# High parts of the first twelve weight blocks: from GpSimd to ScalarE, in a two-layer decoder trunk

## The reference

```python
hn = rms_norm(h, mix_norm[0])
proj = hn @ w_in                      # 1024 x 3584: x, y, q, k, v side by side
x_br, y_br, q, k, v = split(proj)
xc = causal_depthwise_conv(x_br, conv_w, conv_b)      # width 4, per channel
r = sigmoid(block_diag_linear(xc, wa, ba))            # the gates: 4 blocks of 256 x 256
i = sigmoid(block_diag_linear(xc, wx, bx))
```

## Time and profile before

| | us |
|---|---|
| median of 3 runs | 1297.19 (1297.11 to 1297.23) |
| the profiled execution | 1297.3 |
| its span in the trace | 1295.5 |
| TensorE busy | 1286.3 |
| VectorE busy | 921.9 |
| ScalarE busy | 532.5 |
| GpSimd busy | 258.7 |

### The profile page before, as it was taken

How to read it: one execution, slowest core, us unless ns; L and a number is a source line. 1 busy time by engine, 2 the same in 40 slices (tenths; PEclk the granted TensorE clock), 3 DMA queues, 4 the chain that set the end, 5 groups by cost and what they waited for, 6 DMA issues and landing times.

```text
span 1295.5 us, 19991 instructions
## 1 busy us (share of the span) xinstructions
PE 1286.3 (99%) x7554; PEld 1115.4 (86%) x7554; DVE 921.9 (71%) x1458; ACT 532.5 (41%) x1124; POOL 258.7 (20%) x295
## 2 busy tenths in 40 slices
PE   9999999999999999999999999999999999999998
PEld 7778778888888998899988878888888998899986
DVE  8997857446689984388955778557789983489842
ACT  5247356113533560056622347425433550166512
POOL 3111253311422002100021126413321002000010
PEclk9999999999999999999999999999999999999999
DMA  6333323233333333333233332132333323333232
GB/s 236 102 106 113 91 66 98 66 98 98 114 98 98 114 98 98 98 115 98 87 110 114 106 106 69 50 98 88 108 98 98 114 91 94 99 126 98 82 98 98
DMA packets 96701, 130.73 MB, mean 101 GB/s; under 512 B 5312, under 2 KB 61888, under 8 KB 96608
## 3 DMA queue, kind: packets, MB, share of 16 engines
q1 hardware_dynamic: 94976, 127.42, 32.0%
q10 hardware_dynamic: 1632, 2.05, 0.6%
HBM read 124.67 MB, written 2.10 MB: 98 GB/s over the span
## 4 chain that ended last, share of the span: by engine, by line
PE 91%; DVE 5%; issue 2%; DMA 1%; ACT 0%; POOL 0%; SPq 0%; DVEq 0%; POOLq 0%; ACTq 0%
PE ps L784 17%; PE ps L788 16%; PE ps L787 16%; PE ps L942 8%; PE ps L941 8%; PE ps L940 8%; DVE xc L1689 1%; PE ps L1426 1%; PE ps L1427 1%; PE ps L1423 1%; PE ps L1256 1%; PE ps L1272 1%; PE ps L1285 1%; DVE w_lo L1455 1%; PE ps L1145 1%
## 5 line engine op out<-in xcount | busy, mean ns | idle before, releaser
L706 POOL TENSOR_SCALAR w_hi<-raw 128x1024 fp32r<-128x1024 f32 x161 | 184.6, 1147 | 933.9 <-PE ps L942 367.3
L1455 DVE TENSOR_TENSOR w_lo<-raw,w_hi 128x1024 fp32r<-128x1024 f32 x161 | 206.3, 1287 | 178.1 <-POOL w_hi L706 176.2
L784 PE MATMUL ps<-f_hi,w_hi 128*128 128x512 f32 x720 | 281.1, 390 | 1.3 <-ACT small L2312 1.1
L787 PE MATMUL ps<-f_lo,w_hi 128*128 128x512 f32 x720 | 280.2, 389 | 0.0
L788 PE MATMUL ps<-f_hi,w_lo 128*128 128x512 f32 x720 | 280.2, 389 | 0.0
L941 PE MATMUL ps<-zq_lo,quad_hi 128*128 128x256 f32 x896 | 253.6, 283 | 0.0
L940 PE MATMUL ps<-zq_hi,quad_hi 128*128 128x256 f32 x896 | 253.5, 283 | 0.0
L941 PEld LDWEIGHTS ps<-zq_lo,quad_hi 128*128 128x128 f32 x896 | 172.0, 192 | 0.2
L940 PEld LDWEIGHTS ps<-zq_hi,quad_hi 128*128 128x128 f32 x896 | 172.0, 192 | 0.2
L784 PEld LDWEIGHTS ps<-f_hi,w_hi 128*128 128x128 f32 x720 | 135.1, 188 | 30.1 <-ACT small L2312 1.6
L788 PEld LDWEIGHTS ps<-f_hi,w_lo 128*128 128x128 f32 x720 | 135.1, 188 | 28.2
(11 more groups left out here) (267 smaller groups left out, 2042.2 us busy)
## 6 DMA issues: line engine op xcount, KB each, us to landing
quad_raw<-in_w_gate_up SPq DMA_DIRECT2D x64, 512.0 KB
raw<-in_w_down SPq DMA_DIRECT2D x44, 512.0 KB
raw<-in_w_gate_up SPq DMA_DIRECT2D x48, 256.0 KB
raw<-in_w_out SPq DMA_DIRECT2D x20, 512.0 KB
raw<-in_w_in SPq DMA_DIRECT2D x19, 512.0 KB
raw<-in_xa_wkv SPq DMA_DIRECT2D x16, 512.0 KB
raw<-in_w_in SPq DMA_DIRECT2D x18, 256.0 KB, 3.5
raw<-in_xa_wq SPq DMA_DIRECT2D x8, 512.0 KB
```

Source lines behind the costliest of these rows:

```text
L706: pool.tensor_scalar(w_hi[:, slot], raw[:, slot], 1.0, 1.0, ALU.mult, ALU.mult).then_inc(s_hi, 1)
L784: ins = pe.matmul(o, whi, rhi, start=start, stop=False)
L787: pe.matmul(o, whi, rlo, start=False, stop=False)
L1455: dve.tensor_tensor(w_lo[:, slot], raw[:, slot], w_hi[:, slot].bitcast(F32), ALU.subtract).then_inc(s_lo, 1)
```

## The change

GpSimd no longer makes the high parts of blocks 0 to 11; it waits until all twelve are there, and begins with block 12. ScalarE makes them with a Copy, at fixed places in its queue: the two halves of block 0 and the blocks 1 to 4 behind the `z_hi` of the opening, block 5 behind the root of the norm, block 6 behind the first `xc` of the convolution, 7, 8 and 9 behind the second, third and fourth `f_hi`, 10 behind the fifth `xc`, and 11 behind the sixth `f_hi`. VectorE's, TensorE's and SyncE's programs are unchanged. `s_begun` is waited for nowhere in the kernel.

```diff
--- before.py
+++ after.py
@@ -719,13 +719,8 @@
                     high_part(u, u % SLOTS)
 
             first = UNIT0["mixer"]
-            pool.wait_ge(s_raw_first, 16)
-            pool.sem_inc(s_begun, 1)
-            pool.tensor_scalar(w_hi[:, 0, 0], raw[:, 0, 0], 1.0, 1.0, ALU.mult, ALU.mult).then_inc(s_hi_first, 1)
-            pool.wait_ge(s_raw[0], 32)
-            pool.sem_inc(s_begun, 1)
-            pool.tensor_scalar(w_hi[:, 0, 1], raw[:, 0, 1], 1.0, 1.0, ALU.mult, ALU.mult).then_inc(s_hi, 1)
-            high(1, first + 2)
+            pool.wait_ge(s_hi, UNIT0["gates"])
+            high(UNIT0["gates"], first + 2)
             for s in range(STEPS + 2):
                 if s % 3 == 0 and s:
                     normalise_pair(s // 3 - 1, first + s + 2)
@@ -2255,6 +2250,14 @@
 
         @block.scalar
         def _(act):
+            def first_high(half):
+                act.wait_ge((s_raw_first, s_raw[0])[half], (16, 32)[half])
+                act.activation(w_hi[:, 0, half], raw[:, 0, half], ACT.Copy).then_inc((s_hi_first, s_hi)[half], 1)
+
+            def weight_high(u):
+                act.wait_ge(s_raw[u % SLOTS], 32 * (u // SLOTS + 1))
+                act.activation(w_hi[:, u % SLOTS], raw[:, u % SLOTS], ACT.Copy).then_inc(s_hi, 1)
+
             def residual(norm):
 
                 def high(dst, m):
@@ -2270,6 +2273,13 @@
                     else:
                         act.wait_ge(s_h, (NORM[norm] - 1) * DB + m + 1)
                     high(to_hi, m)
+                    if norm == "mix0":
+                        if m < 2:
+                            first_high(m)
+                        elif m % 2:
+                            weight_high((m + 1) // 2)
+                        elif m == 2:
+                            weight_high(1)
                     if m >= 2:
 
 
@@ -2381,7 +2391,9 @@
             act.activation(root[:], ones[:, 0:1], ACT.Sqrt)
             act.wait_ge(s_vec, 16)
             residual("mix0")
+            weight_high(5)
             memory_high(0)
+            conv_turn = {(0, 0): (6,), (0, 2): (7,), (0, 3): (8,), (0, 4): (9,), (4, 0): (10,), (4, 2): (11,)}
             for m0_ in (0, 4):
                 for i in range(5):
                     m = m0_ + i
@@ -2392,6 +2404,8 @@
                     if i >= 1:
                         act.wait_ge(s_xc, m)
                         act.activation(f_hi[:, m - 1, :], xc[:, m - 1, :], ACT.Copy).then_inc(s_xch, 1)
+                    for u in conv_turn.get((m0_, i), ()):
+                        weight_high(u)
             memory_root()
             act.wait_ge(s_sp_e, 1)
             act.activation(small[:, 16:24], small[:, 8:16], ACT.Exp).then_inc(s_sp_e, 1)
```

## The result

| | before | after |
|---|---|---|
| median of 7 runs each, us | 1297.19 (1297.0 to 1297.27) | 1301.65 (1299.8 to 1303.21) |
| the profiled execution, its span | 1297.3, 1295.5 | 1301.09, 1299.3 |
| mean granted clock of the runs | 1.0 in the profiled one | 0.997 to 0.999 |
| restart of TensorE with the gates' blocks | 76.77 | 79.21 |

The ratio is 1.0034 with an interval of 1.0024 to 1.0043: the change makes the kernel 0.34% slower, 4.5 us. The forecast was 1299.2 us, and its range ended at 1301.0. The time is that of the first rival, 1301.7 us, to which 0.10 had been given.

What follows compares the result with a forecast made beforehand. VectorE's queue was taken to bound the kernel up to TensorE's restart at 76.77 us. Terms -2.4 + 5.8 - 2.3 + 0.9 = +2.0 us gave a median of 1299.2 us from 1297.19, range 1297.8 to 1301.0.

Steps and rivals of the forecast that it cites:

- the first rival: At TensorE's restart: clock falls to half after the gap, about eleven matmuls slower, 2.5 us more, 1301.7 us; chance 0.10.
- What bounds the kernel: Up to TensorE's restart at 76.77 us, VectorE's queue sets the time; any shift there passes whole to the end.
- Part 1: Opening: VectorE freed from collisions with GpSimd's copies, so the norm's reciprocal comes at 27.5 us instead of 29.94, -2.4 us.
- whose place was called free of charge: Opening, block 1 behind `z_hi` on ScalarE: a TensorE stall of 0 to 0.2 us, covered by slack before the restart.
- Part 2: Convolution: VectorE waits six times for ScalarE's high parts of blocks 6 to 11, together +5.8 us.
- further semaphore steps: At the six convolution waits: one more semaphore step each, 0.03 to 0.24 us, together +0.2 to +1.4 us.
- collisions of blocks 7 to 11: Convolution: VectorE no longer held up by GpSimd's copies of these blocks, -2.3 us.
- Part 3: GpSimd's copies from block 12 on start later, at about 67.1 us, and meet VectorE's convolutions, +0.9 us.
- The sum on the restart: TensorE's restart with the gates' blocks comes +2.0 us later, at about 78.8 us.
- The failed step: From restart to end: the restart's shift passes on whole, nothing added, 1299.3 us profiled and 1299.2 us median.
- The named signs: Profile after: no GpSimd instruction before 66 us, `z_lo` 0.74 us, six VectorE waits, gap near 3.7 us, later rows merely shifted.

Runs made afterwards that it cites:

- 2: Changed kernel with only the opening's part: ScalarE makes blocks 0 to 5, GpSimd makes 6 to 11 as before; 1295.81 us, ratio 0.9989.
- 4: Changed kernel with ScalarE's blocks 6 to 11 earlier in its queue, ahead of its next wait for VectorE; 1294.43 us, ratio 0.998.
- 9: Changed kernel with four wide matmuls (512 columns) filling TensorE's gap before the gates' blocks; 1300.01 us, ratio 1.0022.
- experiment 10: Changed kernel with 7 small matmuls in TensorE's gap before the gates' blocks; 1300.83 us, ratio 1.0027.
- experiment 5: Kernel before with two further chained copies on ScalarE ahead of the roots, delaying the restart; 1298.55 us, ratio 1.0013.
- experiment 8: Changed kernel with block 10's high part moved right behind block 9's on ScalarE; 1299.76 us, ratio 1.0018.
- experiment 3: Changed kernel with only the convolution's part: GpSimd makes blocks 0 to 5 as before, ScalarE makes 6 to 11; 1302.5 us, ratio 1.004.
- experiments 1: Changed kernel with 14 small matmuls filling TensorE's gap before the gates' blocks; 1300.57 us, ratio 1.0026.
- 7: Kernel before with four delaying copies on ScalarE ahead of the roots and 14 small matmuls in TensorE's gap; 1301.09 us, ratio 1.0029.

## Why the prediction was off, step by step

- **What bounds the kernel: right.** Only the restart counted, it was VectorE's queue that set it, and its shift went to the end whole (2, 4 and 9 in the table).
- **Part 1, opening, -2.4: nearly.** The reciprocal came 2.14 us earlier (27.80, predicted 27.5). All `z_lo` took 0.74 or 0.75 us. What is missing, 0.3 us, was lost at block 1, whose place was called free of charge. TensorE's timeline in the kernel after shows its two passes there, with 1.25 and 1.03 us to the next one instead of 0.91, 0.46 us together:

```profile
10.98 1.19 PE L825 MATMUL ps<-z_hi,w_hi 128*128 128x512 f32 x4
12.23 1.19 PE L835 MATMUL ps<-z_hi,w_lo 128*128 128x512 f32 x4
```

The prediction let the slack before the restart cover such a stall. It doesn't: the norm's sum stands further back in TensorE's own queue, the reciprocal waits for it, and with the reciprocal begins VectorE's queue, which sets the restart. In experiment 10, with x late, TensorE lost 1.3 us at the same place.
- **Part 2, six waits, +5.8: right.** They were 0.52, 1.05, 1.05, 0.26, 1.98 and 1.04 us, less the 0.24 that block 10's low part had before: 5.66. The idle times leave out that a low part which needn't wait starts 0.09 us before the end of the instruction ahead of it; from start to start the six places are 6.1 us dearer than in a kernel without the waits. So the further semaphore steps that the range allowed for (0.2 to 1.4 us) cost 0.3 at most. The collisions of blocks 7 to 11 went as reckoned, -2.3 (all low parts at 1.22 or 1.23 us, all taps at 2.31 to 2.33 but the one of the next point).
- **Part 3, +0.9: right in size.** Taps 3.19 for 2.33 and low part 2.07 for 1.22 are 1.71 us, against 0.92 that blocks 12 to 14 cost before: +0.8.
- **The sum on the restart, +2.0: it was +2.44.** From reciprocal to restart it was +4.58 (6.1 - 2.3 + 0.8), predicted +4.4; the other 0.3 us are the reciprocal's. The gap was predicted at 3.7 us and was 3.4; TensorE's stall before block 11 at about 1 and was 1.4.
- **The failed step: the time was the restart's alone.** "So 1299.3 for a profiled one" passes the restart's shift on at a full clock. The clock's fall stood only among the rivals, with 0.10, on the ground that no row of the trace has a restart after a longer gap. But the sum itself put such a gap there, three times as long as the longest in the trace; to have no row for it was a reason for doubt in the forecast, not for a small chance. The rival's price, 2.5 us for eleven matmuls, was about 1.5 us for seven in the profile, 1.6 to 2.0 in the median, and 0.2 to 3.6 in the single runs. That the rival's 1301.7 us is the measured time to 0.1 us is luck: its restart was 0.4 us too early, its price about as much too high for the median. Of the Trainium skill (TensorE: Matmul & The Clock Gate, "What's actually happening"), which the rival named, the trace now agrees that the clock is halved behind an idle stretch and comes back with busy time (0.50 from 80 to 82 us, 1.00 from 84); the two groups of experiment 5 fit that it isn't the same in each execution, but no run here shows the phase itself. With this term in the sum it would have been 1299.2 + 1.6 to 2.0, about 1301.
- **The range** left this case out as the last tenth; so the time fell 0.65 us outside. Without the clock's fall, 1299.6 to 1300.0 us, it would have been inside.
- **The named signs.** No GpSimd copy before 66 us, `z_lo`, the six waits and the longest of them, the gap, the same rows after 110 us: all seen. The sign of the first rival, matmuls at 0.45 us and a granted clock under 1, was seen as well (0.43 and 0.50).

## What to carry to other kernels

When an engine takes over a job that another one waits for, put it in the queue as early as its data allows, ahead of that engine's next wait and not behind it: the same twelve copies cost 4.5 us in the one order and gain 2.8 in the other. And when a change lets TensorE stand still longer than anywhere in the trace, put the clock into the sum: behind a gap of 3.4 us came 1.5 to 2 us more than the restart's own delay. If the gap can't be closed, a few unneeded matmuls in it keep the clock; look at the later waits too, since the small ones brought a new one of about 1 us.

## What the runs showed of the hardware

- The granted clock fell to half behind gaps of 3.33 to 3.71 us in all four profiles and, by the times, in 26 of 30 executions; behind 2.52 us in the profile and, by the times, in four of eleven; it stayed full in the profiles with 1.22 us or less, and in the one with 1.83. The stretch at half clock cost 1.4 to 2.5 us in the profiles. In three of the five it began while TensorE stood still, in experiment 8 within 0.1 us of the restart, in experiment 3 only after two matmuls at full clock.
- It accounts for most of the scatter of the runs, not for all: 3.4 us in the kernel after and 0.8 with wide fillers, but 1.1 and 2.4 us in experiments 1 and 7, with a full clock.
- Unneeded matmuls of 512 columns (four of them, 3.5 us) and of 128 columns (fourteen, 3.3 us) both kept the clock full.
- With 14 small fillers TensorE met a wait of 0.9 to 1.1 us for a transfer of q some 730 us later, in both kernels that have them; with 4 wide or 7 small ones it didn't, though the restart was later still. Why stays open: no run separates the fillers' number from where they push the transfers.
- A GpSimd copy of 128x1024 and a VectorE instruction with two SBUF inputs that met still cost VectorE time: 3.19 us for three taps of 2.33, 2.07 for a low part of 1.22. GpSimd's copy sometimes paid as well (1.48 instead of 1.05 us) and sometimes not (1.05 at 57.12 us before, beside the low part of 1.86). The one-input copy of `acc` was held up too, 0.84 us instead of 0.42, beside a GpSimd copy in the kernel before. ScalarE's copies of the same size (1.04 or 1.05 us) held no VectorE instruction up: the low parts of blocks 3 and 5 and three `z_lo` that ran beside them took 1.22 or 1.23 and 0.75 us.
